# Routed expert passes ahead of the overflow branch, with a sixth slot for expert weights

## What is computed

```python
hp = modulate(rmsnorm(xp, g_ffn[l]), mp[3], mp[4])
xp = xp + mp[5] * moe(hp, router_w, router_b, moe_w1[l], moe_w3[l], moe_w2[l])

def moe(h, router_w, router_b, w1, w3, w2):      # 16 experts in 4 groups, 1024 -> 256 -> 1024
    scores = sigmoid(t @ router_w)               # best group of 4, then the best 2 experts in it
    hid = silu(t @ w1[e]) * (t @ w3[e]) * combine[:, e]
    return sum over e of hid @ w2[e]
```

## Time and profile before

| | us |
|---|---|
| median of 3 runs (lowest to highest) | 809.03 (808.85 to 813.53) |
| the profiled execution, its own time | 811.42 |
| its span | 809.6 |
| PE busy in the span | 664.1 (82%) |
| DVE, ACT, POOL busy | 226.3, 158.8, 32.1 |
| DMA: 214.75 MB, mean rate | 265 GB/s |
| chain that ended last: PE, DMA, DVE, issue | 71%, 13%, 8%, 5% |

### The profile page before, as it was taken

The page is one execution under the profiler, slowest core; times in us unless marked ns, Lnnn a source line. Parts: engine busy times, 40 slices in busy tenths (PEclk is TensorE's granted clock), DMA queues, the critical chain, the costliest instruction groups (busy, mean ns, idle before and its releaser), DMA issues.

```text
span 809.6 us, 11360 instructions
## 1 busy us (share of the span) xinstructions
PE 664.1 (82%) x4802; PEld 344.7 (43%) x4802; DVE 226.3 (28%) x554; ACT 158.8 (20%) x313; POOL 32.1 (4%) x76
## 2 busy tenths in 40 slices
PE   5599999998899619999674689999996299996705
PEld 3455656557655213333223445466652133332203
DVE  0414104464512561131100440010425611311026
ACT  3111000253411412111100340130004111111012
POOL 1000000000000001000000100000000010000020
PEclk9899999999999769999987699999998699999867
DMA  8993030879954335999978896254733359999652
GB/s 369 428 410 141 23 130 1 342 283 422 373 199 156 155 132 178 377 414 429 428 292 330 318 428 264 99 197 186 298 155 156 133 181 376 421 428 426 272 181 79
DMA packets 23962, 214.75 MB, mean 265 GB/s; under 512 B 2752, under 2 KB 4576, under 8 KB 12000
## 3 DMA queue, kind: packets, MB, share of 16 engines
q1 hardware_dynamic: 13680, 182.06, 55.1%
q0 software_dynamic: 4320, 15.73, 5.6%
q10 hardware_dynamic: 5904, 16.14, 5.0%
HBM read 199.62 MB, written 14.30 MB: 264 GB/s over the span
## 4 chain that ended last, share of the span: by engine, by line
PE 71%; DMA 13%; DVE 8%; issue 5%; ACT 1%; POOL 0%; SPq 0%; DVEq 0%; ACTq 0%; POOLq 0%
PE bank L1322 27%; PE bank L1586 15%; PE bank L1601 6%; DMA work<-in_moe 5%; PE bank L1672 5%; DMA ring<-in_ev_in 4%; PE bank L1262 3%; DVE work L800 3%; DMA ring<-in_ada_w 2%; PE bank L1366 2%; PE bank L1293 2%; PE bank L1459 1%; PE bank L1267 1%; PE bank L1653 1%; DVE rstd L826 1%
## 5 line engine op out<-in xcount | busy, mean ns | idle before, releaser
L1586 PE MATMUL bank<-ring,work 128*32 128x512 f32 x960 | 135.8, 616 | 22.2 <-issue 22.2
L1322 PE MATMUL bank<-hT,ring 128*128 128x384 f32 x416 | 137.7, 492 | 1.8 <-DMA ring<-in_ev_in 1.8
L1322 PEld LDWEIGHTS bank<-hT,ring 128*128 128x128 f32 x416 | 79.2, 192 | 56.5 <-DMA ring<-in_ev_in 2.0
L1322 PE MATMUL bank<-work,ring 128*128 128x384 f32 x256 | 83.4, 487 | 0.3 <-DVE work L800 0.3
L1586 PEld LDWEIGHTS bank<-ring,work 128*32 128x32 f32 x960 | 35.4, 113 | 88.0 <-issue 88.0
L1601 PE MATMUL bank<-ring,work 128*32 128x512 f32 x480 | 65.4, 595 | 2.9 <-ACT work L684 2.9
L1322 PEld LDWEIGHTS bank<-work,ring 128*128 128x128 f32 x256 | 48.3, 190 | 34.6 <-DVE work L800 1.4
L1262 PE MATMUL bank<-ring,csil 128*32 128x128 f32 x1024 | 36.5, 302 | 16.9 <-DMA ring<-in_ada_w 16.9
L1143 DVE COPY work<-bank 128x512 f32<-128x512 f32 x18 | 12.5, 692 | 127.1 <-PE bank L1571 127.1
L1586 PE MATMUL bank<-work 128*32 128x512 f32 x192 | 46.9, 614 | 0.0
L1672 PE MATMUL bank<-ring,hT 128*128 128x512 f32 x96 | 43.3, 612 | 2.1 <-ACT hT L573 2.1
(11 more groups left out here) (185 smaller groups left out, 643.2 us busy)
## 6 DMA issues: line engine op xcount, KB each, us to landing
ring<-in_moe SPq DMA_DIRECT2D x26, 2048.0 KB, 9.6
ring<-in_ada_w SPq DMA_DIRECT2D x16, 3072.0 KB, 14.6
ring<-in_moe SPq DMA_DIRECT2D x26, 1024.0 KB, 14.5
work<-in_moe SPq DMA_DIRECT2D x6, 2048.0 KB, 13.7
ring<-in_ev_in SPq DMA_DIRECT2D x3, 3072.0 KB, 26.0
y_slots<-work ACTq DMA_DIRECT2D x18, 512.0 KB, 11.2
ring<-in_gm_in SPq DMA_DIRECT2D x4, 2048.0 KB, 17.1
work<-in_moe SPq DMA_DIRECT2D x6, 1024.0 KB, 17.0
```

What stands on the lines that cost most here:

```text
L1322: mm = pe.matmul(ps[:, 0:T], w[:, k, j * P:j * P + P], x[:, k, :], start=(k == 0), stop=(k == KD - 1))
L1586: mm = pe.matmul(bank[p % 2][rows, :], h_slotT[:, p % 2, k * P + BLOCK * n:k * P + BLOCK * n + BLOCK], held(place_of(e))[:, k * 512:k * 51 ...
```

## The change

The routed passes run with no condition. Each of PE, ACT and DVE loads `most_i` behind them (PE behind ada 11's rows and turn, ACT behind the scalings, DVE ahead of the sums) and, if it is over 0, redoes the whole mixture in a small loop: h fetched back from `h_all`, one expert at a time through SPARE. POOL has no branch. The index of the gather is clamped to the 1152 places.

`HELD` is 6: the sixth slot, LATE, overlays hT, sq, rstd, logit_t, acc and part of ada_row, now one tensor `state`. Expert 5, the first of the sorted ones, is loaded into it after SP's register reads, once the last rows of h are transposed. `order_experts` moves ahead of the move and the choices of `place`; the choices for the later passes (`later_places`) and the second table (`tokens` on PE, `later_tokens` on DVE) move into the passes, behind turn_h(0).

Of the ada chunks only 11 is loaded ahead of `s_sent`, into SPARE, after expert 10. `s_sent` now holds back gm_in 0. The order behind it is gm_in 0, ada 12, gm_in 1, ada 13, gm_in 2, ada 14, gm_in 3, ada 15; ada 12 to 15 are all computed behind norm(2) and inside the gMLP.

```diff
@@ -40,8 +40,7 @@
 BLOCK = 32
 CAPS = [96] * 6 + [64] * 8 + [32] * 2
 FIXED = SLOTS + 1
-HELD = SLOTS + 1
-ROUNDS = NE // HELD
+HELD = SLOTS + 2
 SORTED = NE - FIXED
 PLACE_AT = [sum(CAPS[:j]) for j in range(NE)]
 PLACES = sum(CAPS)
...
 
 CHUNKS = ([("ada", n) for n in range(3)] + [("ev_in", c) for c in range(3)] + [("ada", 3), ("ada", 4), ("qkv", 0)]
           + [("ada", n) for n in range(5, 11)] + [("ev_out", c) for c in range(2)] + [("moe", (0, e)) for e in range(NE)]
-          + [("ada", n) for n in range(11, 14)]
-          + [("gm_in", 0), ("gm_in", 1), ("ada", 14), ("gm_in", 2), ("ada", 15), ("gm_in", 3)]
+          + [("ada", 11)] + [key for n in range(4) for key in (("gm_in", n), ("ada", 12 + n))]
           + [("gm_out", c) for c in range(2)] + [("moe", (1, e)) for e in range(NE)])
-SPARE = SLOTS
+SPARE, LATE = SLOTS, SLOTS + 1
 
 
 def homes():
...
 
-    home, turns, before, last, r = {}, [0] * (SLOTS + 1), {}, {}, 0
+    home, turns, before, last, r = {}, [0] * HELD, {}, {}, 0
     for key in CHUNKS:
         kind, i = key
         place = i[1] % HELD if kind == "moe" else 0
-        s = SPARE if place == SPARE else (r + place) % SLOTS
+        s = SPARE if key == ("ada", 11) else place if place >= SLOTS else (r + place) % SLOTS
         home[key] = s, turns[s]
         turns[s] += 1
         before[key], last[s] = last.get(s), key
-        if kind != "moe" or i[1] == NE - 1:
+        if kind != "moe" and s < SLOTS:
             r += 1
     return home, before
...
@@ -103,7 +101,7 @@
 
 def dispatch_products(l):
     return ([("router", l), ("logits", l)] + [("h_row", l, t, c) for t in range(NT) for c in range(2)]
-            + [("slots", l)] + [("table", l, g) for g in range(len(TABLES))])
+            + [("slots", l), ("table", l, 0)])
 
 
...
@@ -117,11 +115,12 @@
        + ([("probs_t", s - 1, 0), ("probs_t", s - 1, 1)] if 1 <= s <= HEADS else [])
        + ([("attend", s // 2 - 1)] if s >= 3 and s % 2 else [])]
     + [("mix_out", 0, d) for d in range(KD)] + [("norm", 1)]
-    + dispatch_products(0) + [("ada_row", 11), ("ada_row", 12), ("ada_t", 11), ("ada_t", 12)]
-    + [("moe_t", 0, d) for d in range(KD)] + [("norm", 2), ("ada_row", 13)]
-    + [("gm_v", t, 0) for t in range(NT)] + [("ada_row", 14), ("ada_t", 13)] + [("gm_v", t, 1) for t in range(NT)]
-    + [("ada_t", 14)] + [("gm_u", j) for j in range(4)] + [("ada_row", 15)] + [("gm_u", j) for j in range(4, 6)]
-    + [("ada_t", 15)] + [("gm_u", j) for j in range(6, KD)] + [("spatial", g) for g in range(KD)]
+    + dispatch_products(0) + [("ada_row", 11), ("ada_t", 11)]
+    + [("moe_t", 0, d) for d in range(KD)] + [("norm", 2), ("ada_row", 12)]
+    + [("gm_v", t, 0) for t in range(NT)] + [("ada_row", 13), ("ada_t", 12)] + [("gm_v", t, 1) for t in range(NT)]
+    + [("ada_row", 14), ("ada_t", 13)] + [("gm_u", j) for j in range(4)] + [("ada_t", 14)]
+    + [("gm_u", j) for j in range(4, 6)] + [("ada_row", 15)] + [("gm_u", j) for j in range(6, KD)]
+    + [("ada_t", 15)] + [("spatial", g) for g in range(KD)]
     + [("mix_out", 1, d) for d in range(KD)] + [("norm", 3)] + dispatch_products(1)
...
         xT = sb("xT", [P, KD, T])
-        hT = sb("hT", [P, KD, T])
+        state = sb("state", [P, SLOT + P])
+        hT = state[:, 0:KD * T].rearrange("p (a b) -> p a b", b=T)
...
+        ada_row = state[:, (KD + 7) * T:(KD + 7) * T + 4 * P].rearrange("p (a b) -> p a b", b=2 * P)
...
+            return spare if s == SPARE else late if s == LATE else ring[:, s, :]
 
         def wait(eng, s, value):
...
                 kind, i = key
-                if key == ("ada", 13):
+                if key == ("gm_in", 0):
...
                     load_first(l, j)
+                b, turn = bank_of(("h_row", l, NT - 1, 1))
+                sp.wait_ge(full[b], turn + 1)
                 sp.wait_ge(s_order, l + 1)
                 for j in range(FIXED, NE):
                     place_expert[l, j] = sp.value_load(order_i[0:1, l, j - FIXED:j - FIXED + 1], min_val=0, max_val=NE - 1)
+                load_up(l, FIXED)
+                load_down(l, FIXED)
                 for p in range(PASSES):
                     for j in finished(p):
...
 
-                for g, (first, _) in enumerate(TABLES):
-                    if p == first:
-                        key = ("table", l, g)
-                        pool.wait_ge(taken[bank_of(key)[0]], takes(key))
+                if p == TABLES[0][0]:
+                    key = ("table", l, 0)
+                    pool.wait_ge(taken[bank_of(key)[0]], takes(key))
+                if p == TABLES[1][0]:
+                    pool.wait_ge(s_later[l], 1)
                 if p >= 2:
...
                 pool.wait_ge(s_hstored, 16 * NT * (l + 1))
-                for p in range(2):
+                for p in range(PASSES):
                     fetch(l, p)
-                pool.wait_ge(s_most, l + 1)
-                excess = pool.value_load(most_i[0:1, l:l + 1], min_val=0, max_val=T)
-                with pool.If(excess < 1):
-                    for p in range(2, PASSES):
-                        fetch(l, p)
-                    gather(l)
-                    for c in range(2):
-                        for t in range(NT):
-                            pool.wait_ge(s_back[l][c][t], 16)
-                    sent(l, 0)
-                with pool.Else():
-                    for n in range(SENT):
-                        sent(l, n)
+                gather(l)
+                for c in range(2):
+                    for t in range(NT):
+                        pool.wait_ge(s_back[l][c][t], 16)
+                sent(l, 0)
...
+                for t in range(NT):
+                    act.wait_ge(s_back[l][1][t], 16)
+                act.wait_ge(s_scaled[l], NT)
+                for t in range(NT):
+                    act.dma_start(second[:, t, :], h_all[t * P:t * P + P, :]).then_inc(s_grow[l], 16)
+                for k in range(KD):
+                    act.wait_ge(s_gturn[l], k + 1)
+                    act.activation(hT[:, k, :], bank[k % 2][:, 0:T], ACT.Identity).then_inc(s_ght[l], 1)
+                with act.Fori(0, NE) as e:
+                    act.wait_ge(s_gdown[l], e * NT + 1)
+                    act.dma_start(spare, a["moe"][l, bass.ds(e, 1)].rearrange("a p n -> p (a n)")).then_inc(s_gw[l], 16)
...
                     act.wait_ge(s_back[l][0][t], 16)
                     act.activation(moe_out[:, t, :], moe_out[:, t, :], ACT.Identity, scale=weight[:, l, 0, t:t + 1])\
                         .then_inc(s_scaled[l], 1)
-                if l == 0:
-                    ada(12)
...
             def moe(l):
+                experts_routed(l)
                 act.wait_ge(s_most, l + 1)
                 excess = act.value_load(most_i[0:1, l:l + 1], min_val=0, max_val=T)
                 with act.If(excess > 0):
                     experts_all(l)
-                    if l == 0:
-                        ada(11, 12)
-                with act.Else():
-                    experts_routed(l)
 
             squares(1)
...
@@ -746,11 +741,10 @@
                 for t in range(NT):
                     take(act.activation(v_rows[:, t, c * 512:c * 512 + 512], product("gm_v", t, c)[:, :], ACT.Gelu),
                          "gm_v", t, c)
-                if c == 0:
-                    ada(14)
+                ada(13 + c)
             for j in range(KD):
                 take(act.activation(uT[:, j, :], product("gm_u", j)[:, 0:T], ACT.Gelu), "gm_u", j)
-                if j == 3:
+                if j == 5:
                     ada(15)
...
-            def tokens(l, g):
-
-                first, last = TABLES[g]
-                take(dve.tensor_copy(table[:, l, first:last], product("table", l, g)[:, 0:last - first]), "table", l, g)
+            def tokens(l):
+
+                first, last = TABLES[0]
+                take(dve.tensor_copy(table[:, l, first:last], product("table", l, 0)[:, 0:last - first]), "table", l, 0)
+
+            def later_tokens(l):
+
+                first, last = TABLES[1]
+                dve.wait_ge(s_table[l], 1)
+                dve.tensor_copy(table[:, l, first:last], bank[7][:, 0:last - first]).then_inc(s_later[l], 1)
 
...
-                tokens(l, 0)
+                tokens(l)
                 sort_experts(l)
-                own = s_own[:, :].rearrange("p (t j) -> p t j", t=NT)
+                order_experts(l)
                 cube = move(three(s_tmp))
                 step(cube[0])
-                step(dve.tensor_reduce(own, cube[1], AX.X, ALU.add))
+                step(dve.tensor_reduce(s_own[:, :].rearrange("p (t j) -> p t j", t=NT), cube[1], AX.X, ALU.add))
+
+            def later_places(l):
...
+
+                own = s_own[:, :].rearrange("p (t j) -> p t j", t=NT)
                 for run in RUNS:
                     choose(l, *((run[0], three(s_tmp)) if run[0] < FIXED else (run[0] - FIXED, own)), run)
-                order_experts(l)
-                tokens(l, 1)
-
...
+                later_tokens(l)
```

(74 more changed lines are left out.)

200 lines of the change are left out of this document (68 added, 132 removed).

## The result

The changed kernel takes **783.1 us** (median of 5 runs, 779.0 to 786.0) against 809.6 us for the kernel before in the same comparison: a ratio of **0.966, 95% interval 0.9635 to 0.9685**. The forecast was 777.5 us, range 765 to 790. So the direction and the range held, and the likeliest value was 5.6 us too optimistic. The profiled execution has a span of 777.2 us against 809.6, 32.4 us less.

What follows compares the result with a forecast made beforehand. Bound by TensorE in the fast passes and by late weight transfers at their end, after a bus idle at the start. 12.9 + 12.9 + 11.1 - 2 - 3.4 = 31.5 us off the 809.0 median gives 777.5 us, range 765 to 790.

Steps and rivals of the forecast that it cites:

- The start: Start of each layer's passes: without the branch, first turn_h 7.94 and 6.15 us earlier; net gain 7.2 and 5.4 us.
- rival at 791 us: Passes don't start earlier because the 5.72 and 4.13 us are not the branch: 791 us, chance 0.12.
- The sixth expert's load: Ahead of the passes: issued near 299.8 us on an idle bus, costing the next load at most 0.4 us.
- Landing of the last expert: Ahead of pass 8, layer 0: expert 15 lands at 396.2 instead of TensorE resuming at 409.17, leaving a 4.3 us wait.
- From there to the last y store: Pass 8's start to the last y store: kept at 18.8 us; passes gain 12.9 us in layer 0, 11.1 in layer 1.
- Layer 0's tail: Last y store to moe_t: with the bus empty, 17.4 us instead of 30.3, gaining 12.9 us.
- Ada 12: Norm 2, between moe_t and gm_v: ada 12 loaded second arrives late, costing 2 us, bounds 0 and 3.
- One more chunk in the gMLP: Inside the gMLP, where TensorE never waits: one more ada chunk's rows and turns cost 3.4 us.
- The branch behind the passes: The new If on TensorE, DVE and ScalarE behind the passes: costs nothing, bounds 0 and 5 us a layer.
- The rival at 787 us: The new branch shows: refetched code passes ScalarE's 6.66 us of cover by 4.8 us in both layers; chance 0.13.
- Starvation (835): TensorE starved of instructions behind the branch, in norm and gMLP: 58 us, 835 us; slower cases together 0.03.
- The wait ahead of pass 8 did not vanish: Judges a rival: TensorE's wait for the last expert vanishes altogether, 12.6 us more gain, 765 us, chance 0.13.

Runs made afterwards that it cites:

- two branch runs: Changed kernel with a register load and never-taken branch put back on TensorE ahead of the passes, skipping 60 or 350 transposes: 782.6 and 786.3 us.
- second profile: The changed kernel, unaltered, run and profiled once more: 783.8 us, ratio 0.967, profiled span 783.3 us.
- without the gate: Changed kernel without the wait on s_sent ahead of the gMLP's loads: 797.5 us.
- sixth expert later: Changed kernel with six slots, but expert 5's load waits until up(0) of pass 0 is done: 787.9 us.
- ada 12 first: Changed kernel with ada 12 loaded ahead of gm_in 0, the wait for the gathered rows moved to ada 12: 780.0 us, ratio 0.962.
- sooner: Changed kernel where SP reads only expert 5's register, issues its load, then reads the other ten: 782.3 us, ratio 0.966.

## Why the forecast was right, and where it was off

**The start: right.** First `turn_h` 7.69 us sooner after the table in layer 0 (7.94 forecast) and 6.22 in layer 1 (6.15). The two branch runs show that the 5.72 and 4.13 us were the branch. Its rival at 791 us is out. The sixth expert's load went out 10.77 us after the table (10.6 forecast), the next one 17.97 us after it (17.6). That the bytes of such a pair are through 2 us before it lands is not what the kernel before shows (they moved until some 0.6 us before), but nothing hung on it: the load behind was held by up(0). By the Trainium skill ("Runtime: NRT & Kernel Launch", Instruction fetch mechanics) a taken branch stalls when its target lies outside the prefetched pages; 0.35 us over 60 transposes and 5.0 us over 350 are in line with that.

**Landing of the last expert: right; the wait was mis-sized.** Forecast 396.2 us. Measured 372.43 + 21.8 = 394.2, and 1.9 us of the difference lie ahead of the layer, so 396.1 on the forecast's clock. The forecast of a 4.3 us wait failed on its other end: it took 399.1 - 7.2 = 391.9 for the end of the work ahead; on that clock it came at 390.7, since the 1.25 us wait ahead of pass 7 went too. Hence 5.64 us. The longer wait itself cost nothing, as the landing sets the time.

**From there to the last y store: 1.0 us short in layer 0.** Forecast 18.8, measured 414.23 - 394.43 = 19.80; the first 32 matmuls took 6.28 us at the clock that had fallen in the wait, 5.03 in the kernel before. In layer 1 19.16 against 19.2. Together with a start of pass 8 that came 0.15 us later on the forecast's clock this is the difference between 13.0, which the forecast's own figures give (it wrote 12.9), and 11.85.

**Between two executions: not foreseen.** The second profile has 1.0 us less gain in layer 0's passes and 1.7 less in layer 1's. Over half of that is how long the clock took to rise in up(0), the rest the landing of the last expert and the slow matmuls behind it. The forecast took both from one execution and gave them no loss; the kernel before had 4.15 and 5.09 us for the same 32 matmuls, so part of the first profile's gain in layer 1 (4.20 us) is luck.

**Layer 0's tail: mechanism right, a reading wrong, 0.7 to 1.9 us too large.** The prediction put three ada loads (9 MB) ahead of the last y store of the kernel before. Rows 7 merge three issues; the timeline up to 425 us has two at that time (6 MB), and the third went out at 456.02, behind the store:

```profile
421.64 0.81 SPq L406 DMA_DIRECT2D ring<-in_ada_w  x2
```

The second of the two landed after 20.1 us, at about 442.2, and the store at 428.00 + 14.6 = 442.6, so the mechanism stands with 6 MB. That the gain is the free bus, the 33.97 us without the gate show. The tail took 18.06 and 19.34 us where layer 1's 17.4 had been taken over. In the five variants in which the bus has the same to carry there (sixth expert later, both branches, ada 12 first, sooner) it took 17.28 to 18.81 us, and over all seven it goes with the landing of the last store: 2.72 us in the shortest tail, 4.76 in the longest. Why that store was late in some is open; ada 11 had landed 4.3 us before it was issued in the first profile (389.37 + 20.5 = 409.9).

**Ada 12: 3.0 to 3.4 us, taken as 2, upper bound 3.** Counted from `moe_t`, the loads were released 1.2 us ahead (1.9 forecast), ada 12 went out 0.4 us behind the release and landed after 14.86 us (14.9), so 14.1 us behind `moe_t` (13.0). The mechanism held, the size didn't: the landing was 1.1 us later, and 3 us of rows and turn had been taken at the full clock; they took 4.2 us, since the clock had fallen in the wait (0.62 in the stretch above). Together that is more than the 0.8 us of wait which the forecast's own figures gave and the 2 us that it took.

**One more chunk in the gMLP: 1.7 us, taken as 3.4.** The rows and the turn took the 3.4 us that were forecast, to within 0.2. The forecast missed that the rows of ada 12, directly ahead of `gm_v`, take the fall of the clock upon themselves: 20.99 us for the first half instead of 22.50 (20.80 in the second profile). With ada 12 first the 1.4 us are lost again.

**The branch behind the passes: right, nothing.** On TensorE 0.43 and 0.85 us, under the gather; on ScalarE and DVE 0.05 to 0.07 us; ScalarE's wait ahead of the squares in layer 1 is 6.70 us (6.66 before), the tail there 17.85 and 17.63 against 17.42. The rival at 787 us is out by its mechanism, although the median came within 4 us of its price. Starvation (835) is out: no "issue" gap stands in the gMLP, whose first half takes 20.99 us, less than before.

**The wait ahead of pass 8 did not vanish** (765). What decides it is the order of the queue: with 2 MB moved behind expert 15's up part it falls to 0.52 / 1.75 us.

Summed by the second profile: 3.5 us less than forecast in the passes (2.1 and 1.4), 1.9 in the tail, 1.4 for ada 12, 0.2 in layer 1's tail, 7.0 together, against 1.7 more in the gMLP and 0.1 around: 31.5 - 7.0 + 1.8 = 26.3 us. No single step failed; the terms that came out short had been sized from one execution each, the large ones at landing times. That the likeliest value was missed by only 5.6 us owes something to luck: 7.0 us of optimism met 1.7 us from a saving in `gm_v` that it had not foreseen.

What stays open: how the price of the branch grows between 60 and 350 skipped transposes, and how much of the 783 could be had with both orders of the queue chosen together (ada 11 later, for instance), which wasn't tried.

## What to carry over

When the bus sets the end of a stretch, look first at what lies in its queue ahead of the bytes that are needed next: moving 2 MB behind them was worth 12 us here, nearly half as much as the whole change. A load that is issued sooner helps only while the bus would be idle and the one behind it is not held by something else; moving the first load 4 us ahead brought nothing. And a forecast that takes each landing time and each slow stretch behind a wait from one execution should allow for their spread: two profiles of the same kernel differed by 6.1 us. Merged rows of a timeline ("x3" over 34.71 us) have to be taken apart before bytes are counted from them.
